# Four column groups per ada_w load, and a long convolution over four residues of positions

## What is computed

```
mod = silu(c) @ ada_w + ada_b                      # 1024 x 6144, for c and for c_ctx
h = rmsnorm(x, norm_mix_w) * (1 + scale) + shift
proj = h @ w_in                                    # Hyena part 3 x 512, mLSTM part 4 x 512 + 16 gates
# Hyena: u = dwconv(proj[:1536]); x0, x1, v = split(u); v = v * x1
k = filter from a small sine MLP over positions, times a decay, divided by sum(abs(k))
y = irfft(rfft(v, n=2L) * rfft(k, n=2L))[:L]       # L = 1024 (latent) and 128 (prompt), 512 channels
y = (y + hy_bias * v) * x0
```

## Time and profile before

| | us |
|---|---|
| median of 3 runs | 1914.91 (1909.60 to 1915.44) |
| the profiled execution | 1913.99 |
| its span, first to last instruction | 1912.2 |
| PE busy in it | 1720.9 |
| DVE busy | 1023.5 |
| ACT busy | 478.0 |
| POOL busy | 485.3 |
| mean granted clock of PE, of 2.4 GHz | 0.945 |

### The profile page before, as it was taken

One profiled execution on the slowest core, in us unless ns is written; L12 is line 12 of the kernel. 1 busy time (PEld: TensorE's weight loads), 2 busy tenths in 40 slices (PEclk: granted clock), 3 DMA queues, 4 the chain that ended last, 5 costly groups with the idle time before them and its releaser, 6 DMA issues. The chain is left out here.

```text
span 1912.2 us, 22738 instructions
## 1 busy us (share of the span) xinstructions
PE 1720.9 (90%) x9631; PEld 1521.9 (80%) x9631; DVE 1023.5 (54%) x1354; ACT 478.0 (25%) x614; POOL 485.3 (25%) x196
## 2 busy tenths in 40 slices
PE   6988699999999992695993999999999999999997
PEld 1327588898888992684993999999999999999996
DVE  4331623336651235595114588288468558648856
ACT  1322521223222214345223222122112122112202
POOL 1322321032230002670053133132123122222230
PEclk8999799999999996796996999999999999999999
DMA  6754401243335356336400211101111111101102
GB/s 192 256 200 175 140 28 49 89 160 126 113 139 168 123 205 192 102 99 236 138 1 0 67 45 45 45 23 45 45 45 45 45 45 44 45 23 45 45 23 111
DMA packets 126378, 179.66 MB, mean 94 GB/s; under 512 B 9404, under 2 KB 92852, under 8 KB 123204
## 3 DMA queue, kind: packets, MB, share of 16 engines
q1 hardware_dynamic: 124847, 175.80, 27.5%
q10 hardware_dynamic: 1428, 2.40, 0.4%
HBM read 144.55 MB, written 33.63 MB: 93 GB/s over the span
## 5 line engine op out<-in xcount | busy, mean ns | idle before, releaser
L233 PE MATMUL psum<-ffn_h_hi,w_hi 128*128 128x320 f32 (+1 forms) x1104 | 261.1, 340 | 25.2 <-PEq L261 25.2
L2652 DVE SCALAR_TENSOR_TENSOR w_raw<-psum,par,w_raw 128x945 f32<-128x945 f32 (+2 forms) x176 | 214.7, 1220 | 90.2 <-ACT w_raw L2599 86.5
L235 PE MATMUL psum<-ffn_h_lo,w_hi 128*128 128x320 f32 (+1 forms) x1104 | 260.5, 339 | 0.0
L237 PE MATMUL psum<-ffn_h_hi,w_lo 128*128 128x320 f32 (+1 forms) x1104 | 260.3, 339 | 0.0
L2652 DVE SCALAR_TENSOR_TENSOR mlp_acc_a<-psum,par,mlp_acc_a 128x945 f32<-128x945 f32 (+2 forms) x176 | 214.5, 1219 | 56.3 <-ACT mlp_acc_a L2599 53.1
L2535 POOL TENSOR_TENSOR w_lo<-w_raw,w_hi 128x2048 fp32r<-128x2048 f32 x32 | 148.0, 4624 | 306.5 <-ACT w_hi L2529 306.5
L233 PEld LDWEIGHTS psum<-ffn_h_hi,w_hi 128*128 128x128 f32 x1104 | 179.8, 188 | 42.7 <-issue 25.5
L237 PEld LDWEIGHTS psum<-ffn_h_hi,w_lo 128*128 128x128 f32 x1104 | 179.9, 188 | 16.6
L235 PEld LDWEIGHTS psum<-ffn_h_lo,w_hi 128*128 128x128 f32 x1104 | 179.9, 188 | 16.5
L2676 DVE SCALAR_TENSOR_TENSOR tail_x<-psum,mod,tail_x 128x384 f32<-128x384 f32 x192 | 94.9, 515 | 128.3 <-PE psum L237 128.2
L235 PE MATMUL psum<-mlp_g_lo,w_hi 128*128 128x384 f32 x480 | 161.3, 336 | 0.0
(11 more groups left out here) (332 smaller groups left out, 2851.9 us busy)
## 6 DMA issues: line engine op xcount, KB each, us to landing
filt_ada<-ada_w SPq DMA_DIRECT2D x24, 1024.0 KB, 5.2
w_raw<-ffn_w_up SPq DMA_DIRECT2D x22, 1024.0 KB, 5.1
w_raw<-w_in SPq DMA_DIRECT2D x14, 1024.0 KB, 5.2
w_raw<-ffn_w_down SPq DMA_DIRECT2D x11, 1024.0 KB, 5.0
scan_rows_spread<-scratch_scan_rows SPq DMA_DIRECT2D x36, 256.0 KB, 3.7
w_raw<-k_fwd SPq DMA_DIRECT2D x8, 1024.0 KB, 6.0
oproj_y<-scratch_y SPq DMA_DIRECT2D x8, 576.0 KB, 5.7
rownorm_x<-x_sample SPq DMA_DIRECT2D x8, 512.0 KB, 8.1
```

Of the source, the lines that this page charges most:

```text
L233: ins = nc.tensor.matmul(out, wh, x_hi(k, i), start=begin, stop=False)
L235: ins = nc.tensor.matmul(out, wh, x_lo(k, i), start=False, stop=False)
L237: ins = nc.tensor.matmul(out, wl, x_hi(k, i), start=False, stop=end)
L2652: ins = stt(out=out, in0=image(up_at)[:, r0 + dy:r1 + dy, c0 + dx:c1 + dx], scalar=weight(i, loc, t), in1=out, op0=ALU.mult, op1=ALU.add)
```

## The change

1. **ada_w** is loaded as 24 parts of 128 rows by 2048 columns, with a ring of four. The four groups of 512 columns of a part are multiplied by four matmuls whose outputs lie on partitions 0, 32, 64 and 96 of one bank. Eight parts complete 2048 columns; ACT copies four pairs of rows, and four full transposes turn them, three times in all. The number of matmuls stays 96, with 512 columns each. The parts are dealt out anew between the other work.
2. **The transforms** use frequencies k + 1/2 and positions parted by their residue modulo 4. A tile of 128 frequencies gives four tiles' worth by sums and differences, so there are two units of matrices instead of four, and each sum runs over two position tiles instead of four. The filter's spectrum takes 12 groups of 24 matmuls of 256 columns in place of 4 of 48 (and 9 with 512 columns for the shared rows); `sums` takes 24 of 256 columns in place of 24 of 512, as does `back` 1 to 8. DVE does the butterflies: four operations on 2 x 256 elements more ahead of the fold's products, and more behind them. The work for the shared row goes.
3. Two units of k_fwd fewer are loaded in `kt` and in `proj`, and two of k_inv fewer in `proj`; x is loaded in one go.

```diff
-    PARTS, AW, RING = 24, 512, 3
+    PARTS, AW, RING = 24, 512, 4
+    SIDES, TURN_AT = 4, (2, 7)
...
-        sizes = [1, 2, 2] + [2] * (NT - 1) + [3]
+        sizes = [2, 4, 3] + [1, 1, 1, 2, 2, 2, 2, 2] + [2]
...
-                    for k in range(HK * (p % 2), HK * (p % 2) + HK):
-                        last = nc.tensor.matmul(ps[0:2, ADA_BANK + q % 2, :], cond[:, k, :], cols(ada[:, p % RING, :], AW)[:, k % HK, :],
-                                                start=(k == 0), stop=(k == KD - 1))
+                    for side in range(SIDES):
+                        last = nc.tensor.matmul(ps[32 * side:32 * side + 2, ADA_BANK + g % 2, :], cond[:, k, :],
+                                                ada[:, p % RING, side * AW:(side + 1) * AW], start=(k == 0), stop=(k == KD - 1))
...
+            for g in range(12):
+                kt, half = STEPS4[g // 3]
+                ring.ready(pe, kt + 1)
+                if g == 2:
+                    pe.wait_ge(prompt_read, 1)
+                if g >= 4:
+                    pe.wait_ge(read, g - 3)
+                on = slice(HC2 * half, HC2 * half + HC2)
+                for i in range(2):
+                    for q in range(2):
...
+                        last = product(nc, [pair(g)[:, i, HC2 * q:HC2 * q + HC2]],
+                                       lambda t: wh[:, 8 * sine + 2 * r + t, :], lambda t: wl[:, 8 * sine + 2 * r + t, :],
+                                       lambda t, _: x_hi[:, x, 2 * r + t, on], lambda t, _: x_lo[:, x, 2 * r + t, on], range(2))
...
+def butterflies(step, tt, out, t):
+    step.do(tt(out[:, 0:5:4, :], t[:, 0:6:5, :], t[:, 1:5:3, :], ALU.add))
+    step.do(tt(out[:, 1:6:4, :], t[:, 0:6:5, :], t[:, 1:5:3, :], ALU.subtract))
+    step.do(tt(out[:, 3:7:3, :], t[:, 2:4, :], t[:, 6:8, :], ALU.add))
+    step.do(tt(out[:, 2:8:5, :], t[:, 2:4, :], t[:, 6:8, :], ALU.subtract))
...
                 for i in range(2):
-                    pairs = [(i, NT - 1)] if h == 0 else [(4 * i + t, 4 * i + t) for t in range(4)]
-                    last = product(nc, [ps[:, 6 + i, :]], lambda a: ch[:, a[0], :], lambda a: cl[:, a[0], :],
-                                   lambda a, _: v_hi[:, a[1], :], lambda a, _: v_lo[:, a[1], :], pairs)
+                    for q in range(2):
+                        r = residue(sine, i, q)
+                        last = product(nc, [ps[:, 6 + i, q * (DH // 2):(q + 1) * (DH // 2)]], lambda t: ch[:, 2 * r + t, :],
+                                       lambda t: cl[:, 2 * r + t, :], lambda t, _: v_hi[:, 2 * r + t, on],
+                                       lambda t, _: v_lo[:, 2 * r + t, on], range(2))
...
-                pe.wait_ge(i_lo_done, 1 if g == 0 else 3 if g <= CH else 5)
+                pe.wait_ge(i_lo_done, 1 if g == 0 else 2 if g <= CH else 3)
...
+                if at_ == 0:
+                    dve.wait_ge(spectrum_out, 16)
+                butterflies(step, tt, vs[:], cross[:])
+                dve.wait_ge(k_in, 16 * (at_ + 2))
...
+                first, second = t[:, 0:8:2], t[:, 1:8:2]
+                step.do(tt(vs[:, 0:4], first, second, ALU.add))
+                step.do(tt(vs[:, 4:8], first, second, ALU.subtract))
+                a, b = vs[:, 0:3:2], vs[:, 1:8:6]
+                step.do(tt(t[:, 0:3:2], a, b, ALU.add))
+                step.do(tt(t[:, 1:4:2], a, b, ALU.subtract))
+                a, b = vs[:, 4:7:2], vs[:, 3:6:2]
+                step.do(tt(t[:, 4:8:3], a, b, ALU.add))
+                step.do(tt(t[:, 5:7], a, b, ALU.subtract))
                 dve.sem_inc(folded, 1)
```

More of the change, by code:

```diff
@@ L1620, in _ @@
             sp.wait_ge(spec_out[1], 32)
-            for u in range(5, 7):
+            for u in range(3, 5):
                 sp.wait_ge(ring.raw_in[ring.slot(u)], 16 * (u // 2))
@@ L1625, in _, with halves @@
         def _(pool):
-            for u in range(2, 5):
-                ring.split_lo(pool, u)
+            ring.split_lo(pool, 2)
         @blk.tensor
         def _(pe):
-            transform_products(nc, pe, mem, ring, x_hi, x_lo, True, full, prompt_read, row_done, spec_done)
+            def halves(u):
+                return [a.rearrange("p (b k) -> p b k", k=P) for a in (ring.hi(u), ring.lo(u))]
+            ring.ready(pe, 0)
+            wh, wl = halves(0)
+            for i in range(2):
+                last = product(nc, [pair(2)[:, i, :]], lambda k: wh[:, i, :], lambda k: wl[:, i, :],
+                               lambda k, _: x_hi[:, i, NT - 1, :], lambda k, _: x_lo[:, i, NT - 1, :], range(1))
@@ L1633, in _ @@
         @blk.scalar
         def _(act):
[L1635 to L1646 removed]
+            ring.split_hi(act, 2)
@@ new lines, in _ @@
+            for g in range(12):
+                n = g // 3
+                act.wait_ge(full, g + 2)
+                if n and g % 3 == 0:
+                    act.wait_ge(spec_done, n)
+                if n and g % 3 == 2:
+                    act.wait_ge(read, g - 2)
+                nc.scalar.activation(low_part(g).rearrange("p a c -> p (a c)"), pair(g)[:, 1, :], ACT.Copy).then_inc(odd, 1)
+                if g % 3 == 2:
+                    if n >= 2:
+                        norm.take_root(act, n - 2)
+                    if n >= 1:
+                        norm.squares(act, n - 1)
@@ new lines, in _ @@
+            for g in range(12):
+                n = g // 3
+                bank, low = pair(g)[:, 0, :].rearrange("p (a c) -> p a c", c=HC2), low_part(g)
+                dve.wait_ge(odd, g + 1)
+                if g % 3 < 2:
+                    m = g % 3
+                    step.do(tt(parts[:, 4 * m:4 * m + 2, :], bank, low, ALU.add))
+                    tt(low[:, m, :], bank[:, m, :], low[:, m, :], ALU.subtract).then_inc(read, 1)
+                    continue
+                tt(parts[:, 3:7:3, :], bank, low, ALU.subtract).then_inc(read, 1)
+                dve.wait_ge(read, g + 1)
+                if n >= 2:
+                    dve.wait_ge(spec_out[n % 2], 16)
+                butterflies(step, tt, spec[:, n % 2], parts)
+                dve.sem_inc(spec_done, 1)
+                if n >= 2:
+                    norm.scale(dve, n - 2)
+                if n >= 1:
+                    norm.mean(dve, n - 1)
```

403 lines of the change are left out of this document (172 added, 231 removed).

## The result

The changed kernel takes 1833.69 us (median of 4 runs, 1832.5 to 1837.56), the kernel before 1912.74 us beside it: a ratio of 0.9591, 95% interval 0.9567 to 0.9614. That is 79 us faster; the forecast was 1821, the range 1804 to 1864. The profiled execution's span is 1832.7 us (before 1912.2).

What follows compares the result with a forecast made beforehand. PE was taken as the bound, busy for 1720.9 of 1912.2 us. First phase 41.3, filter spectrum 25.0, forward transform 3.5 and inverse 24.2 make 94 us off 1913.99, so a median of 1821 us, range 1804 to 1864.

Steps and rivals of the forecast that it cites:

- The first phase: Stretch up to `kt`: overlapping ada_w matmuls leave the transfers as the limit, so it ends at 98.8 instead of 140.1 us, −41.3.
- my bounds of 0.87 and 3.5: ada_w in the first phase: us for a part's four matmuls, at best one matmul's time, at worst as before the change.
- the transfers are then the limit: First phase: any part time up to 2.8 us gives the same sum, set by loads at 368 GB/s.
- The filter's spectrum: `kt`: fewer and narrower matmuls and a shorter tail make it 48.6 instead of 73.6 us, −25.
- The forward transform: `sums` in `proj`: PE saves 22.3 us, but the fold's chain behind it leaves only −3.5.
- 4.8 us of wait at three places: `sums` in `proj`: PE waits this long for c_lo each time, as the longer fold's chain ends after PE is there.
- The inverse: Backs in `proj`: 1 to 8 save 2.8 us each and the 3.0 us wait for i_lo goes, −24.
- About 1.2 come back at the end: End of `proj`: us lost because the last block's load, finish and store, ahead of the w_out loads, don't shrink with PE.
- what lies behind `proj` stays: Everything after the projection: claimed to keep its time, no change.
- No overlap: Rival, first phase: the four ada_w matmuls run one after another, −3 instead of −41, 1859 us; chance 22%.
- The fold's chain doesn't bind: Rival, `sums` in `proj`: PE's saving arrives less 4 at the end, −18 instead of −3.5, 1806 us; chance 8%.
- Quarter use lets the clock fall and nothing overlaps: Rival, first phase: ada_w records take 0.853 us each at 1.2 GHz, +80 there, 1942 us; chance 4%.

Runs made afterwards that it cites:

- e5: Changed kernel with seven of eight ada_w parts writing to one same quarter, the eighth to four (modulation not computed): 1852.9 us in one run.
- e10: Changed kernel with the modulation's first four transposes behind the fourth w4 product instead of the third: 1831.72 us, ratio 0.9571.
- e1: Changed kernel with the old ada_w treatment (24 loads of 512 by 512, outputs on partitions 0 and 1), new transforms kept: 1870.96 us, ratio 0.9793.
- e2: Changed kernel with a part's four matmuls all on one quarter, the next part on the next (modulation not computed): 1845.3 us, ratio 0.9652.
- e4: Changed kernel with the w_out loads issued at item 28, ahead of the last stores and the last y_raw load: 1830.0 us, ratio 0.9578.
- e7: Changed kernel with the w_out loads behind the last y_raw load (item 29) and their split at item 30, beside PE's work: 1820.72 us, ratio 0.9511.
- e6: e3 plus an earlier load of k_fwd's second unit (item 14) and the sum's copy ahead of the next w_hi: 1819.77 us, ratio 0.9506.
- e3: Changed kernel with c_hi made on ACT ahead of silu and w_hi, c_lo on POOL ahead of w_lo: 1830.55 us, ratio 0.9576.
- e8: Changed kernel with the moves of e6 and e7, and i_hi and y_hi ahead of w_hi on ACT at item 20: 1810.74 us, ratio 0.9459.
- e9: Changed kernel with the moves of e6 and e7, and the prompt's inverse (back 0) a place later, inside item 22: 1807.14 us, ratio 0.9447.
- e12: Changed kernel with all moves of e9 and that of e10: 1804.09 us, ratio 0.9431.

## Why the prediction was right or wrong

**The first phase: right, with luck: two errors cancel.** Forecast −41.3, measured −39.4 (−39.4 to −42.1 over the eight profiles); the last part's matmuls began at 88.1 us, where I had its landing at 87.5. The overlap is real: 1.04 us for a part, near the lower of my bounds of 0.87 and 3.5, where e5 gives 3.5. Of "the transfers are then the limit" only half is true. They ran at 397 to 398 GB/s, not at my 368, in two of three windows; in the third PE was the limit, at 1.2 GHz and with 297 GB/s. The faster transfers would have saved 4.9 us on the 23.3 MB (my estimate, by 398 instead of 368 GB/s). The step that I left out was the clock: I had costed PE's parts at 2.4 GHz because the old phase kept 1.00 from 48 to 113 us, but PE waited only once there, for 0.4 us, and in the new phase it waits eleven times for a part, and for ACT's copies. That these waits bring the clock down is not shown; in e10 it fell without the longest of them, of 2.8 us. What the clock costs within the eight profiles is small: with 0.57 from 48 to 72 us the spectra begin at 100.2 to 100.6, with 0.87 at 98.0 to 98.2. The Trainium skill (DMA: Bandwidth & Descriptors, "Specifications") has 358 GB/s for a core's share of HBM, by which the last part would have come 1.8 us later, and 435 GB/s for the fabric; a single busy core here is well above the first and below the second.

**The filter's spectrum: right.** Forecast −25, measured −25.6.

**The forward transform: wrong, and half hidden by luck.** Forecast −3.5, measured +0.2. From the start of `proj` to the end of the last `sums` it is 334.7 before and 330.9 us after, −3.8 where my pieces made −7.5; from there to the end of back 0, 31.4 and 35.4, +4.0 as forecast. But 3.3 of the −3.8 lie ahead of the first `sums` (200.7 to 197.4), where PE's work and its waits are the same before and after and the kernels with the change take 196.5 to 200.0; why the one profile of the kernel before has 200.7 stays open. The stretch that my pieces were about, from the first to the last `sums`, went from 134.1 to 133.5 us, −0.5. Up to the end of the second `sums` it shrank by 5.2 us (forecast 5.6), but the three pairs behind, which I had at −0.3, −0.8 and −0.8, became longer by 1.9, 1.5 and 1.3 us (from end to end). Two terms of the sum were too small. I expected 4.8 us of wait at three places and measured 7.1, 4.9 and 4.7, 2.3 more in all (and 8.9 for the prompt's y_lo, as forecast). And I had no term for the `sums` behind each wait: PE came out of it at 1.2 GHz and took 4.6 us instead of 3.0, 4.8 us in all. In the prediction a wait cost only itself.

**The inverse: right.** From back 0's end to the last product 143.3 us before, 119.3 after: −24.0, where I had −25.4 without the end. The wait for i_lo went, the backs took 3.0 us from first to last record.

**The end of the projection: the step that failed.** "About 1.2 come back at the end" and "what lies behind `proj` stays": measured +11.9 in this profile, and 28.8 to 35.1 us of gap in the five profiles in which `proj` is as the change left it (changed, e1, e2, e5, e10), 31.9 on average or +8.7. So some 3 of the 11.9 us are this profile's own. I named the chain (load, finish, store, then w_out) and its 13 us, and took it for shorter than it is. Counted from the end of back 5, PE's last product came 7.6 us sooner (59.0 to 51.4) while the last store came 7.9 us later (44.4 to 52.2), since the cycles of 12.3, 12.4 and 13.2 us became 14.3, 15.1 and 15.5. This shifts the loads by 15.4 us against PE; 5.0 us of slack were there (w_out would have landed at 718.8, 9.9 us after its issue, against 723.8). 15.4 − 5.0 makes 10.4, and ACT waited 10.3. Without the loads at this place (e4, e7) the gap is 22.9 and 22.1.

**The rivals.** No overlap (1859 us): refuted by the 1.04 us; e5 shows 1853 in one run with an eighth of the parts overlapped. Its sum had the new treatment without overlap at −3 where it is about −10. The fold's chain doesn't bind (1806): refuted, c_lo was waited for at three places; but e6 shows that 13.5 us could be had from the stretch of the `sums` by order alone. Quarter use lets the clock fall and nothing overlaps (1942): refuted, they overlap; the clock did fall for a time.

**Sum.** −39.4 − 25.6 + 0.2 − 24.0 + 11.9 = −76.9, and 2.6 us less behind the restart (that stretch is 1162 to 1168 us in all profiles): −79.5 of span, against −94. Of the 14.5 us between them, 10.7 are the end, 3.7 the forward transform (7.0 short in its own stretch, less the 3.3 ahead of it), 1.9 the first phase and 1.4 the inverse; 0.6 of `kt` and the 2.6 go the other way.

## What to carry to other kernels

Where a change takes work off the main engine, list every chain of loads and stores that runs beside it at fixed length, and work out for each by how much it ends ahead of that engine now: what the engine gains beyond that slack is lost. Waits of TensorE cost more than themselves where the work behind them begins at half the clock: here 1.6 us more for each of three waits of 4.7 to 7.1 us. Shorter waits cost this only at times: of the thirteen of 0.9 to 2.7 us ahead of a `sums` in e3, e6, e8, e9 and e12, nine were followed by one of 3.1 us and four by one of 4.4 to 4.5. When a chain on helper engines binds, first look at what stands ahead of its links in each queue (ACT, POOL and SP here) before shortening the links: three kinds of move (ACT, POOL, SP) took 13.5 us off one stretch, without an operation less. And compare the stretches that an edit doesn't touch: here they differed by up to 6 us between kernels alike, as much as several of the effects looked for.

## What the runs showed of the hardware

- Full float32 matmuls with 2 output rows on four quarters of the array's columns run side by side: 1.04 us for four of 512 columns, against 3.60 on one quarter, 3.5 times as fast. The Trainium skill (TensorEngine Tiling (Array Packing), "Theoretical Speedup") allows up to four times; the trace agrees, a little below that.
- They need not be neighbours in the order: with four matmuls on one quarter and then four on the next, two such parts took 5.32 us instead of 7.03, so the second part ran beside the first for 1.7 us, longer than one matmul of 0.87.
- DVE's subtraction of 128x256 for i_lo took 4.53 us beside POOL's w_lo (503.60 to 508.10 us) and 0.42 us in e8, where POOL was idle. The Trainium skill (SBUF — State Buffer, "Who interferes with whom") says that such an operation of DVE with two inputs in SBUF and one of GpSimd that reads it exclude each other; the rows agree. Removing it gave nothing on the whole: i_hi had to wait for the store of the spectrum and the load behind it, and PE's waits for y_lo came to 10.4 us, against 10.8 in e6.
- The same first phase took 98.0 to 100.6 us in eight profiles, with the clock from 48 to 72 us between 0.57 and 0.88 and the transfers between 297 and 358 GB/s there.
